# Recurrence levels on half the queries, and block 1's low weight parts on VectorE

## What is computed

```python
b = jnp.cumsum(gc, axis=2)                       # running log decay, per key channel
decay = exp(where(incl, b[:, :, :, None, :] - b[:, :, None, :, :], -inf))
scores = einsum('bhtk,bhtsk->bhts', qc, decay * kc[:, :, None, :, :])
o_intra = einsum('bhts,bhsv->bhtv', scores, vc)
```

## Time and profile before

| what | value |
|---|---|
| median of three runs | 1780.9 us |
| the profiled execution: time, and its span | 1782.84 us, 1781.0 us |
| PE busy in the span | 1730.8 us (97%) |
| DVE busy | 951.6 us (53%) |
| ACT busy | 698.4 us (39%) |
| POOL busy | 205.1 us (12%) |
| recurrence stage (995 to 1200 us): PE, DVE, POOL busy | 198.02, 152.91, 72.98 us of 205.00 |

### The profile page before, as it was taken

The page is one execution under the profiler, slowest core; times in us unless marked ns, Lnnn a source line. Parts: engine busy times, 40 slices in busy tenths (PEclk is TensorE's granted clock), DMA queues, the critical chain, the costliest instruction groups (busy, mean ns, idle before and its releaser), DMA issues.

```text
span 1781.0 us, 20994 instructions
## 1 busy us (share of the span) xinstructions
PE 1730.8 (97%) x8107; PEld 1371.6 (77%) x8107; DVE 951.6 (53%) x1709; ACT 698.4 (39%) x1267; POOL 205.1 (12%) x168
## 2 busy tenths in 40 slices
PE   8989999999999999999999999999999999999998
PEld 5558788667888888877788787775887888887887
DVE  4455566444463333357555777665544655556334
ACT  3233344744333322344464555542333422223234
POOL 3242100002000000020000333320200200000000
PEclk9999999999999999999999999999999999999999
DMA  6243202132433323323221111113220232222221
GB/s 193 75 134 95 95 25 74 52 111 73 127 95 96 99 92 105 104 73 106 72 68 52 36 60 36 60 57 141 92 90 24 86 102 96 95 95 95 95 95 48
DMA packets 122372, 152.24 MB, mean 85 GB/s; under 512 B 8827, under 2 KB 110609, under 8 KB 121762
## 3 DMA queue, kind: packets, MB, share of 16 engines
q1 hardware_dynamic: 119986, 140.19, 24.4%
q0 software_dynamic: 2288, 10.71, 1.7%
HBM read 144.90 MB, written 6.00 MB: 85 GB/s over the span
## 4 chain that ended last, share of the span: by engine, by line
PE 90%; DVE 5%; ACT 2%; issue 1%; DMA 1%; POOL 0%; DVEq 0%; ACTq 0%; POOLq 0%
PE bank L1981 50%; PE bank L2015 16%; PE bank L1261 2%; PE bank L1679 2%; PE bank L2237 2%; PE bank L2356 2%; PE bank L2234 1%; PE bank L1212 1%; PE bank L2329 1%; PE bank L774 1%; PE bank L1124 1%; PE bank L1129 1%; PE bank L1713 1%; PE bank L2112 1%; PE bank L2040 1%
## 5 line engine op out<-in xcount | busy, mean ns | idle before, releaser
L1981 PE MATMUL bank<-act_high,w_high 128*128 128x512 f32 x1360 | 552.1, 406 | 8.5 <-DVE act_low L965 2.6
L1981 PE MATMUL bank<-act_high,w_low 128*128 128x512 f32 x1360 | 532.2, 391 | 0.0
L1981 PE MATMUL bank<-act_low,w_high 128*128 128x512 f32 x1360 | 531.2, 391 | 0.0
L643 ACT ACTIVATE w_high<-ring 128x1024 fp32r<-128x1024 f32 x222 | 234.3, 1056 | 672.2 <-PE bank L1981 458.4
L667 DVE TENSOR_TENSOR w_low<-ring,w_high 128x1024 fp32r<-128x1024 f32 x202 | 257.2, 1274 | 220.4 <-ACT w_high L643 220.4
L1981 PEld LDWEIGHTS bank<-act_high,w_high 128*128 128x128 f32 x1360 | 256.2, 188 | 70.2 <-issue 14.6
L1981 PEld LDWEIGHTS bank<-act_high,w_low 128*128 128x128 f32 x1360 | 256.0, 188 | 55.3
L1981 PEld LDWEIGHTS bank<-act_low,w_high 128*128 128x128 f32 x1360 | 256.4, 189 | 51.8 <-issue 4.4
L2015 PE MATMUL bank<-act_high,w_high 128*128 128x512 f32 x416 | 162.1, 390 | 2.3 <-DVE arena L3263 1.2
L2015 PE MATMUL bank<-act_high,w_low 128*128 128x512 f32 x416 | 161.9, 389 | 0.0
L2015 PE MATMUL bank<-act_low,w_high 128*128 128x512 f32 x416 | 161.9, 389 | 0.0
(11 more groups left out here) (372 smaller groups left out, 2230.3 us busy)
## 6 DMA issues: line engine op xcount, KB each, us to landing
ring<-in_ffn_w SPq DMA_DIRECT2D x32, 1024.0 KB, 5.3
ring<-in_w_in SPq DMA_DIRECT2D x28, 1024.0 KB, 5.1
ring<-in_w_up SPq DMA_DIRECT2D x22, 1024.0 KB, 5.0
ring<-in_w_down SPq DMA_DIRECT2D x11, 1024.0 KB, 4.8
ring<-in_w_mem_kv SPq DMA_DIRECT2D x8, 1024.0 KB, 5.3
ring<-in_cmp_w SPq DMA_DIRECT2D x4, 1024.0 KB, 7.8
ring<-in_w_out SPq DMA_DIRECT2D x4, 1024.0 KB, 5.6
ring<-in_w_mix_out SPq DMA_DIRECT2D x4, 1024.0 KB, 5.2
```

The lines of the kernel that those rows point to most:

```text
L643: nc.scalar.activation(part(w_high, name), raw_part(name), ACT.Copy).then_inc(w_rounded, 1)
L1981: last = nc.tensor.matmul(b[0:rows, :], w[:, k, 0:rows], a, start=k == 0 and n == 0, stop=k == KT - 1 and n == 2)
```

## The change

From i = 1 on a level's matmul takes as moving operand only the query half of each block, so 64 columns in place of 128 per chunk, and the results of the four chunks lie packed in the first 256 columns of the bank. The selections of DVE and the block copies of ACT read this packed form; DVE's work on 128 x 256 elements in place of 128 x 512. The stationary operand stays the full 128 x 128. In block 1 DVE makes the low parts from `ckv` on (18 of 20), each placed in its list behind the take of the tile two before (`low_behind`). POOL keeps `cq0` and `cq1` and its DMA issues.

```diff
@@ low weight parts
-        next_part = {"act": 0, "pool": 0, "dve": w_part_at["wo0"]}
+        next_part = {"act": 0, "pool": 0, "dve": w_part_at["ckv"]}
@@ def level_scores
-                keys, qs = (G_X[(LEVELS * g + i - 1) % N_X],) * 2 if i else (G_KEY[g % 2], ar(QH + g // 2))
-                last = nc.tensor.matmul(bank[at % 2][:, cs], keys[:, cs], qs[:, cs], start=True, stop=True)
+                if i:
+                    x = G_X[(LEVELS * g + i - 1) % N_X][:, cs]
+                    last = nc.tensor.matmul(bank[at % 2][:, c * HALF:(c + 1) * HALF], x,
+                                            halves(x, i - 1, g % 2)[0], start=True, stop=True)
@@ def level_keep (i >= 1)
-                mask = const(f"lv{'fb'[g % 2]}{i - 1}").bitcast(U32).unsqueeze(1).to_broadcast([P, TT, P])
+                w, q = 1 << (i - 1), 1 - g % 2
+                dst = G_SCORE[g % 2].rearrange("p (c b two w) -> p c b two w", c=TT, two=2, w=w)[:, :, :, q, :]
+                src = bank[at % 2][:, 0:TT * HALF].rearrange("p (c b w) -> p c b w", c=TT, w=w)
+                mask = const(f"lv{'fb'[g % 2]}{i - 1}").bitcast(U32).rearrange("p (b two w) -> p b two w", two=2, w=w)
+                mask = mask[:, :, q, :].unsqueeze(1).to_broadcast([P, TT, HALF // w, w])
                 ins = nc.vector.copy_predicated(dst, mask, src)
@@ gpsimd: its split_weights calls after cq1 go, here two of them
-                split_weights(eng, ("kcvc", "n_q0", "n_q1", "a_c0")[h])
-            split_weights(eng, "s_v1")
@@ vector: 18 calls, here the three that the prediction speaks of
+            def low_behind(name):
+
+                split_on_dve(eng, w_part_at[name] + PAIRS)
+
             take_normed("a_c0", ar(AB))
...
+            low_behind("a_c0")
             eng.wait_ge(bias_out, 128)
             query_rope(0)
             norm_apply(eng, "q1")
             take_normed("a_c1", ar(AB + 1))
+            low_behind("a_c1")
...
             gated_conv(0)
+            low_behind("a_u0")
...
             take_normed("s_k1", ar(SKT + 1))
+            low_behind("s_k1")
             take("vc", vc[0:N_CMP, 64:P], N_CMP, 64)
```

More of the change, by code:

```diff
@@ L664, in split_on_dve @@
                 eng.wait_ge(w_rounded, i + 1)
-                if name == "wo0":
+                if name == "ckv":
                     eng.wait_ge(w_split, i)
@@ L1645, in two_blocks @@
         DVE_LEVELS = 6
+        HALF = P // 2
         def level_kept(eng, at):
@@ L1659, in block_keep @@
             w, d = 1 << (i - 1), g % 2
-            src = bank[(8 * g + i) % 2][:, :].rearrange("p (c t) -> p c t", t=P)
+            src = bank[(8 * g + i) % 2][:, 0:TT * HALF].rearrange("p (c t) -> p c t", t=HALF)
             dst = G_SCORE[d].rearrange("p (c t) -> p c t", t=P)
@@ L1663, in block_keep @@
                 keys, qs = slice(at + w * d, at + w * d + w), slice(at + w * (1 - d), at + w * (1 - d) + w)
-                ins = nc.scalar.activation(dst[keys, :, qs], src[keys, :, qs], ACT.Copy)
+                ins = nc.scalar.activation(dst[keys, :, qs], src[keys, :, at // 2:at // 2 + w], ACT.Copy)
             ins.then_inc(level_act, 1)
@@ L1677, in level_scores @@
                 cs = slice(c * P, (c + 1) * P)
-                keys, qs = (G_X[(LEVELS * g + i - 1) % N_X],) * 2 if i else (G_KEY[g % 2], ar(QH + g // 2))
-                last = nc.tensor.matmul(bank[at % 2][:, cs], keys[:, cs], qs[:, cs], start=True, stop=True)
+                if i:
+                    x = G_X[(LEVELS * g + i - 1) % N_X][:, cs]
+                    last = nc.tensor.matmul(bank[at % 2][:, c * HALF:(c + 1) * HALF], x,
+                                            halves(x, i - 1, g % 2)[0], start=True, stop=True)
+                else:
+                    last = nc.tensor.matmul(bank[at % 2][:, cs], G_KEY[g % 2][:, cs], ar(QH + g // 2)[:, cs],
+                                            start=True, stop=True)
             last.then_inc(level_mm, 1)
@@ L1685, in level_keep @@
             eng.wait_ge(level_mm, at + 1)
-            dst = G_SCORE[g % 2].rearrange("p (c t) -> p c t", t=P)
-            src = bank[at % 2][:, :].rearrange("p (c t) -> p c t", t=P)
             if i == 0:
+                dst = G_SCORE[g % 2].rearrange("p (c t) -> p c t", t=P)
+                src = bank[at % 2][:, :].rearrange("p (c t) -> p c t", t=P)
                 if g >= 2:
@@ L2875, in hidden_silu @@
                 nc.vector.tensor_copy(small[:, 60:61], e[:, 0, 0:1]).then_inc(hid_out, 1)
+            def low_behind(name):
+                split_on_dve(eng, w_part_at[name] + PAIRS)
             take_normed("cq0", ar(CQ))
             take_bias(0, "strip")
+            low_behind("cq0")
             take_normed("cq1", ar(CQ + 1)[0:108], 108)
             take_bias(0, "fwd")
+            low_behind("cq1")
             eng.wait_ge(cols_turned, 2)
@@ L2885, in _ @@
             take_bias(1, "strip")
+            low_behind("ckv")
             taken(eng, "gates")
@@ L2891, in _ @@
             take_bias(1, "fwd")
+            low_behind("nv")
             norm_apply(eng, "ckv")
@@ L2894, in _ @@
             take_bias(2, "strip")
+            low_behind("kcvc")
             taken(eng, "kcvc")
@@ L2901, in _ @@
             take_bias(2, "fwd")
+            low_behind("kskw")
             take_normed("n_q0", ar(AQ))
             take_bias(3, "strip")
+            low_behind("n_q0")
             norm_apply(eng, "kskw")
@@ L2906, in _ @@
             take_bias(3, "fwd")
+            low_behind("n_q1")
             nc.vector.tensor_copy(kc[64:P, 0:N_CMP], ident[64:P, 64:64 + N_CMP])
@@ L2926, in _ @@
             gated_conv(0)
+            low_behind("a_u0")
             query_rope(3)
             gated_conv(1)
+            low_behind("a_u1")
             norm_apply(eng, "mk2")
             conv_gate(0)
+            low_behind("a_b0")
             norm_apply(eng, "mk3")
             conv_gate(1)
+            low_behind("a_b1")
             nc.vector.memset(nv[:, :, 0:5:2, :], 0.0)
@@ L2938, in _ @@
             take_query("s_q0", ar(SQT))
+            low_behind("s_q0")
             norm_apply(eng, "mq1")
             take_query("s_q1", ar(SQT + 1))
+            low_behind("s_q1")
             norm_apply(eng, "mq2")
             take_normed("s_k0", ar(SKT))
+            low_behind("s_k0")
             hidden_silu(1)
```

2 lines of the change are left out of this document (removed).

## The result

| kernel | median of runs | profiled execution (span) |
|---|---|---|
| before | 1781.03 us, 6 runs (1779.31 to 1781.54) | 1782.84 us (1781.0) |
| after | 1785.83 us, 6 runs (1784.76 to 1790.04) | 1785.57 us (1783.8) |

The ratio after to before is 1.0032, 95% interval 1.0019 to 1.0044: slower by some 0.3%, where 1777.1 us was forecast, with a range up to 1782.5. The prediction was wrong in sign.

What follows compares the result with a forecast made beforehand. PE was taken to bound the kernel, with 90% of the chain of waits. The terms 0 - 1.7 - 2.5 + 0.35 = -3.8 us gave 1779.0 us for the profiled execution, 1777.1 against the median; range 1772.5 to 1782.5 us.

Steps and rivals of the forecast that it cites:

- Level matmuls, 0: PE's level passes in the recurrence: 64 columns cost what 128 do, 0 us, bounds 0 and -22.7.
- The earlier end of the last pass, 0.05 us: Recurrence: a level's last pass on PE ends 0.05 us earlier, and so the selection behind it starts earlier.
- Selections 0.47 us for all 40: DVE in the recurrence, i = 1 to 5: each half selection takes 0.47 us in place of 0.75, 0.28 less.
- the broken pattern eats it: DVE's half selections: the lower bound of the saving, 0 us each, if the broken pattern uses it up.
- End keys of five quiet g, -1.7: Recurrence, g = 0, 1, 2, 4, 6: DVE 0.33 us earlier at the end keys PE waits for, -1.7 us in all.
- g = 3, 5, 7, -2.5: Recurrence: PE's waits for level 3's products and the end keys shrink by 0.85 us per g, -2.5 us in all.
- Block 1, +0.35: Low parts moved to DVE: `a_u0` -1.0, `a_b0` +0.3, head of the attention net +1.05, sum +0.35 us.
- the scaling: Head of block 1's attention: 0.30 us instead of 0.96 without POOL's low part beside it; PE's wait shrinks by 0.65.
- Clock, 0 with bounds of 1.7: PE's 1.2 GHz stretches: one at g = 5 may go, one at the attention's head may come; 0, bounds -1.7 and +1.7.
- the recurrence's -4.2: The forecast for the recurrence: -1.7 us for the quiet end keys and -2.5 us for g = 3, 5 and 7.
- The slower rival: DVE's list holds up PE at the head of block 1's attention, clock drops: +2.0 us, 1782.9 us, chance 0.14.

Runs made afterwards that it cites:

- e10: e7 with level products of 128 columns in place of 64; median 1776.49 us against 1781.26 of before, ratio 0.9966.
- e7: e1 with semaphore waits that put POOL's subtractions of levels 4 to 6 behind DVE's products and end keys; 1776.94 us against 1781.35 of before, ratio 0.9982.
- e3: e1 with level products of all 128 columns, so only the selections are halved; 1781.40 us against 1782.79 of before, ratio 0.9986.
- e4: Level products of 64 columns written to their places in the bank, full selections as in before; 1789.47 us against 1782.79, ratio 1.0038.
- e6: e1 with a small memset on POOL ahead of its subtraction, levels 4 to 6 of odd g; 1781.22 us against 1781.35 of before, ratio 0.9994.
- e2_low: Before with only block 1's part of the change, its low weights all on DVE; 1781.65 us against 1782.79 of before, ratio 0.9995.
- e1: Before with only the recurrence's part of the change, block 1 as in before; 1786.58 us against 1782.79 of before, ratio 1.0019.
- e8: Before with only the semaphore order of e7 for POOL's subtractions; 1777.71 us against 1781.35 of before, ratio 0.9980.
- e5: e2_low with the low weights of `s_v1` computed behind the take of `vc`; ratio to before 0.9992.
- e11: e2_low with the low weights of `s_v1` in the first unit of block 1's attention; 1781.25 us against 1781.26 of before, ratio 0.9994.

## Why the prediction was wrong

- **Level matmuls, 0:** right. A pass of 64 columns costs what one of 128 does (levels 2.28 us apart, as against 2.29; e10 against e7, 0.1 us in the sum of seven intervals).
- **The earlier end of the last pass, 0.05 us, "and so the start of the selection behind it":** the step that failed. The same pass also releases POOL's subtraction, and the prediction did not follow that; it put it at nothing. In g=1 the subtraction starts 0.036 us sooner relative to DVE's product (16 ns behind it before, 20 ns ahead after), and each product that loses takes 0.9 us more. Summed over g=1, 3 and 5 the odd intervals grew by 1.19 + 0.85 + 0.86 = 2.9 us. e3, e4 and e6 show it from three sides. g=7 lost the race as well (1.35 us), but only for one product; PE was 0.3 us late by level 4 and got that back from the shorter selection ahead of the end keys, whose wait fell from 0.87 to 0.63 us.
- **Selections 0.47 us for all 40:** 24 of them take 0.44; the 16 of levels 1 and 2 stayed at 0.74 (the lower bound, "the broken pattern eats it"). So DVE had none of the 0.56 us that two selections were to give ahead of the products of level 3.
- **End keys of five quiet g, -1.7:** 0 in the four even ones, and in g=1 the wait grew from 0.27 to 0.64 us. In the even g the time saved went into L1565, held until POOL's subtraction ended. e7 shows it: with POOL behind, the wait goes.
- **g = 3, 5, 7, -2.5:** +0.85, +0.86 and 0.0. The prediction asked who gets in first, and took both answers as gains, of 0.6 or 1.7; it looked at the one product that lost already and not at those that won, by 16 to 29 ns. The rule of the lock that it cited was right, and its use was one-sided.
- **Block 1, +0.35:** right, term by term. `a_u0` gave -0.96 (PE starts at 120.36 us in place of 121.32), `a_b0` cost 0.28, `vc` 1.68 (a wait of 2.29 us in place of 0.61), and the scaling without POOL beside it gave back 0.66: +0.34 together. The clock added little in sum, by luck: the stretch at 121 us was 3.4 us shorter (PE's lead grew from 0.96 to 2.41 us in it), and the new one at 199.9 us cost 1.6 us again. So the profile is 0.4 us late at the recurrence; e2_low is equal to before within its interval.
- **Clock, 0 with bounds of 1.7:** in the recurrence it was +1.2, behind the longer waits of g=3 (e1 and e4 have a stretch there too), in block 1 +0.1, and -1.5 at 1356.6 us, which no run ties to the change.

Together the recurrence's -4.2 became 2.9 + 1.2 - 0.2 = +3.9, where the -0.2 is by how much the even intervals without a new stretch got shorter. The slower rival had a part of it, "DVE's gain at g = 3, 5 and 7 is used up by POOL", but not that POOL could take more than the gain. Its 1782.9 us also lay above the stated range, which was said to take in most of it.

## What to carry to other kernels

When an edit ends an instruction some 50 ns earlier, list everything that instruction releases, on every engine, and look for pairs that start within 0.1 us of each other on VectorE and GpSimd: here a product that won by 16 ns lost 0.9 us once the other side moved by 36 ns. If such a pair lies on the critical path, lay its order down with a semaphore rather than leave it to timing; here that alone was worth 0.2% (e8). And look at what comes behind an operation that is made shorter: the half selection of i = 3, which reads PSUM, gained nothing in the even g, since the copy behind it reads SBUF and then stood beside GpSimd's subtraction for the time saved.

## What the runs showed of the hardware

- A predicated copy of 128 x 256 float32 takes 0.74 us if its target has runs of 1 or 2 elements, and 0.44 in runs of 4 or more. The mask's runs do not matter (0.74 with a contiguous mask, 0.43 with a contiguous target). A product of two SBUF tiles with the same short runs takes 0.42.
- Which of VectorE and GpSimd is first was decided by 14 to 30 ns at level 1, and in before, after, e1 and e3 in the same way in all four odd g. Kernels with the same recurrence agree in their odd intervals: after and e1 to 0.01 us, and e2, e5 and e11, on three chips, to 0.02 us. So such a race repeats from run to run until the program changes. It is not quite clear-cut: in g=7 of e4, with 20 ns between the starts, the one recorded second won.
- The one that is second doesn't always wait alone: where VectorE was first by 16 ns, GpSimd's subtraction took 1.35 us in place of 1.08 (both in g=1, rows above).
- A tensor-scalar operation with one SBUF input (L1516) is held up as well: 0.68 us beside POOL's subtraction in before (rows above), 0.46 without one in after (1024.43 us), and 1.06 in e7.
